# Stick-breaking attention in a two-layer transformer kernel: the causal mask moved from matmuls into the scan, and the values products moved directly behind the scores

## What is computed

```python
rel = query position - key position
strict = rel > 0
z = einsum('bhqd,bhkd->bhqk', q_blk, k) * scale
log_beta = log_sigmoid(z)
log_1mb = where(strict, log_sigmoid(-z), 0.0)
between = cumsum(log_1mb, axis=3, reverse=True) - log_1mb
a = where(strict, exp(log_beta + between), 0.0)
out = einsum('bhqk,bhkd->bhqd', a, v)
```

## Time and profile before

| what | value |
|---|---|
| median of three timed runs | 2841.06 us (2838.6 to 2841.15) |
| profiled execution, first to last instruction (span) | 2839.9 us; the page gives no other time of that execution |
| PE / DVE / ACT / POOL busy | 97% / 58% / 30% / 56% of the span |
| 57 to 336 us (stick-breaking part): PE / DVE / ACT / POOL busy | 271.5 / 168.3 / 136.1 / 161.4 us of 279 |
| mean granted clock of TensorE | 0.990 |

### The profile page before, as it was taken

One profiled execution on the slowest core, in us unless ns is written; L12 is line 12 of the kernel. 1 busy time (PEld: TensorE's weight loads), 2 busy tenths in 40 slices (PEclk: granted clock), 3 DMA queues, 4 the chain that ended last, 5 costly groups with the idle time before them and its releaser, 6 DMA issues.

```text
span 2839.9 us, 38349 instructions
## 1 busy us (share of the span) xinstructions
PE 2742.4 (97%) x13202; PEld 2193.9 (77%) x13202; DVE 1644.7 (58%) x2348; ACT 858.2 (30%) x1696; POOL 1601.4 (56%) x1240
## 2 busy tenths in 40 slices
PE   7999999899999999999999999989999999999998
PEld 5677777676878888887788887767787878888887
DVE  5655577738567777777734302485445355556556
ACT  4544445435321111213413113554233100110102
POOL 3555411355998777776533343222366987777764
PEclk9999999999999999999999999999999999999999
DMA  3322222034211111115411242212424121111134
GB/s 136 102 86 79 87 84 68 23 119 141 82 41 53 56 55 44 59 59 182 167 56 52 74 148 97 82 53 96 171 96 156 37 67 45 53 58 44 59 121 146
DMA packets 76778, 243.77 MB, mean 86 GB/s; under 512 B 7119, under 2 KB 10992, under 8 KB 76276
## 3 DMA queue, kind: packets, MB, share of 16 engines
q1 hardware_dynamic: 54576, 184.31, 19.4%
q10 hardware_dynamic: 22084, 57.86, 5.7%
HBM read 207.00 MB, written 32.52 MB: 84 GB/s over the span
## 4 chain that ended last, share of the span: by engine, by line
PE 81%; DVE 8%; POOL 5%; ACT 3%; issue 2%; DMA 1%; POOLq 0%; DVEq 0%; ACTq 0%; SPq 0%
PE ps L813 17%; PE ps L815 16%; PE ps L814 16%; PE ps L1127 7%; PE ps L1128 7%; PE ps L1129 7%; PE ps L899 2%; PE ps L919 2%; POOL arena L703 1%; PE ps L933 1%; PE ps L1410 1%; PE ps L1422 1%; DVE ps L2489 1%; DVE ps L2506 1%; PE ps L936 1%
## 5 line engine op out<-in xcount | busy, mean ns | idle before, releaser
L639 POOL CAST wh<-raw 128x1024 fp32r<-128x1024 f32 x175 | 186.8, 1067 | 854.4 <-PE ps L815 803.6
L813 PE MATMUL ps<-hh,wh 128*128 128x512 f32 x1456 | 600.6, 412 | 8.1 <-DVE hl L2450 3.6
L815 PE MATMUL ps<-hh,wl 128*128 128x512 f32 x1456 | 572.9, 394 | 0.0
L814 PE MATMUL ps<-hl,wh 128*128 128x512 f32 x1456 | 572.3, 393 | 0.0
L641 POOL TENSOR_TENSOR wl<-raw,wh 128x1024 fp32r<-128x1024 f32 x175 | 422.6, 2415 | 14.0
L729 POOL TENSOR_TENSOR wl<-raw,wh 128x512 fp32r<-128x512 f32 x256 | 344.3, 1345 | 20.5
L813 PEld LDWEIGHTS ps<-hh,wh 128*128 128x128 f32 x1456 | 276.4, 190 | 83.4 <-issue 25.3
L815 PEld LDWEIGHTS ps<-hh,wl 128*128 128x128 f32 x1456 | 275.8, 189 | 60.1
L814 PEld LDWEIGHTS ps<-hl,wh 128*128 128x128 f32 x1456 | 276.6, 190 | 52.7 <-issue 3.4
L813 PE MATMUL ps<-gated,wh 128*128 128x512 f32 (+1 forms) x728 | 279.9, 385 | 3.6 <-DVE gated L2540 3.2
L814 PE MATMUL ps<-gated,wh 128*128 128x512 f32 (+1 forms) x728 | 278.6, 383 | 0.0
(11 more groups left out here) (341 smaller groups left out, 5103.7 us busy)
## 6 DMA issues: line engine op xcount, KB each, us to landing
raw<-weights SPq DMA_DIRECT2D x271, 512.0 KB, 3.5
arena<-w_ada SPq DMA_DIRECT2D x48, 512.0 KB, 3.8
arena<-gate_scratch ACTq DMA_DIRECT2D x20, 512.0 KB, 5.1
arena<-x_t ACTq DMA_DIRECT2D x1, 4096.0 KB, 14.0
x_scratch<-arena ACTq DMA_DIRECT2D x2, 2048.0 KB, 9.0
arena<-x_scratch SPq DMA_DIRECT2D x2, 2048.0 KB, 9.6
gate_scratch<-arena ACTq DMA_DIRECT2D x16, 256.0 KB, 2.1
x_scratch<-arena ACTq DMA_DIRECT2D x1, 4096.0 KB, 12.8
```

The source lines that it names most:

```text
L639: pool.tensor_copy(wh[:, s], raw[:, r]).then_inc(Z.wt_hi, 1)
L813: pe.matmul(out, wh[:, slot, w], xh, start=start, stop=False)
L814: pe.matmul(out, wh[:, slot, w], xl, start=False, stop=False)
L815: return pe.matmul(out, wl[:, slot, w], xh, start=False, stop=stop)
```

## The change

Five edits:

1. The mask products are gone; the scores raise `z_full` themselves. Nothing waits for the mask tile any more in this part of the kernel.
2. A new constant tile `reset` of 128x1024 holds zeros and, in its last 128 columns, the identity. POOL writes it at its start (a memset of 128x896 and a copy of 128x128), ahead of its first split, once the constants are there.
3. The scan is now state = max(u x state, reset), starting at 0, over the keys from right to left. Until the query's own key the state stays 0; there `reset` is 1 and the product starts anew.
4. b is no longer 0 on the last key of the last block, which POOL doesn't multiply. So the last block's values products take 127 keys instead of 128.
5. For stick-breaking steps `a_values` comes directly behind `a_scores`, ahead of the first turn and of fill.

ACT waits once for the mask tile before it stores it for later use. To make room for `reset` in SBUF, the program is created with a DMA scratch of 1024 bytes.

```diff
@@ a_scores (PE)
-                if s == 0:
-                    pe.wait_ge(Z.s_mask, 2)
                         last = pe.matmul(bank(2 * side, 2)[:, c:e], Q_T[i % 2][r, query(s)], K_T[i % 2][r, c:e],
-                                         start=True, stop=(i >= SB_JOBS), skip_group_check=True)
-                        if i >= SB_JOBS and e == w:
+                                         start=True, stop=True, skip_group_check=True)
+                        if e == w:
                             last.then_inc(Z.z_full, 1)
-                if i < SB_JOBS:
-                    for side in range(2):
-                        pe.matmul(bank(2 * side, 2)[:, w - P:w], masks[:, 0], masks[:, 1], start=False, stop=True,
-                                  skip_group_check=True).then_inc(Z.z_full, 1)
@@ a_values (PE)
+                        keys = slice(0, P - 1 if k == b else P)
-                            last = pe.matmul(bank(5)[r, 0:P], HV[i % 2][:, k, r], S_AT[side][s % 2][:, kt],
+                            last = pe.matmul(bank(5)[r, 0:P], HV[i % 2][keys, k, r], S_AT[side][s % 2][keys, kt],
@@ the loop over steps (PE)
                 if s < A_N:
                     a_scores(s)
+                beside = s in VALUES_AT and VALUES_AT[s] < SB_N
+                if beside:
+                    a_values(VALUES_AT[s])
...
                     a_turn(TURN_AT[s], *turning[0])
-                if s in VALUES_AT:
+                if s in VALUES_AT and not beside:
                     a_values(VALUES_AT[s])
@@ POOL, ahead of the first split
+            pool.memset(reset[:, 0:S - P], 0.0).then_inc(Z.s_reset, 1)
+            pool.wait_ge(Z.consts, 32)
+            pool.tensor_copy(reset[:, S - P:S], mat("ident")).then_inc(Z.s_reset, 1)
@@ ACT, ahead of the store of the masks
+            act.wait_ge(Z.s_mask, 2)
@@ s_remain (DVE)
-                v = S_U[u % 3][:, 0:width(s)][:, ::-1]
+                v, ends = S_U[u % 3][:, 0:width(s)][:, ::-1], reset[:, S - width(s):S][:, ::-1]
+                if u == 0:
+                    dve.wait_ge(Z.s_reset, 2)
                 dve.wait_ge(Z.s_u, u + 1)
-                dve.tensor_tensor_scan(v, v, v, 1.0, ALU.mult, ALU.min).then_inc(Z.s_c, 1)
+                dve.tensor_tensor_scan(v, v, ends, 0.0, ALU.mult, ALU.max).then_inc(Z.s_c, 1)
@@ kernel
-    nc = bacc.Bacc("TRN2", target_bir_lowering=False, num_devices=1)
+    nc = bacc.Bacc("TRN2", target_bir_lowering=False, num_devices=1, dynamic_dma_scratch_size=1024)
```

More of the change, by code:

```diff
@@ L156, in build @@
         dsm = place("dsm", [P, 64])
+        reset = place("reset", [P, S])
         ps = ctx.enter_context(nc.psum_tensor("ps", [P, 8 * HALF], F32))
@@ L181, in build @@
         f_half f_ev t_full t_free z_full pv_full o_ev
-        mask_in s_mask s_u s_b s_c s_a d_near d_max d_nmx d_exp d_r d_m d_w
+        mask_in s_mask s_reset s_u s_b s_c s_a d_near d_max d_nmx d_exp d_r d_m d_w
         o_sq o_rs o_norm o_hi o_lo l7_hi l7_lo
```

## The result

The changed kernel takes 2822.41 us (median of 5 runs, 2822.22 to 2824.14), the kernel before 2841.06 us (5 runs, 2836.18 to 2843.83): 18.65 us less, a ratio of 0.994 with an interval of 0.9929 to 0.9951. The forecast was 2826.3 us, with a range of 2820 to 2835.

The account below looks back on a forecast made before the run. PE, busy 97% of the span, was taken to bound the kernel. Masks 8.3, order 4.5 and stalls 2.0 sum to 14.8 us; 2839.9 - 14.8 + 1.2 = 2826.3 us, range 2820 to 2835.

Parts of the forecast that it names:

- PE bounds the stage, and the time follows what it issues: Stick-breaking stage: PE, busy 271.5 of 279 us, sets the time; 14.8 us saved there, the rest shifts whole.
- Masks, 8.3 us: Stick-breaking steps on PE: dropping a pair of mask products saves its 0.277 us slot in 30 steps, 8.3 us.
- Order, 4.5 us at the changes of form and 2.0 at the stalls: Values ahead of the turn: 0.16 us in 28 steps, plus 0.65 us at the turns of steps 9, 17 and 25.
- The rule that a change of tiling mode drains the engine: PE in values steps: one of four mode changes a step goes, a saving; the rule gives no price.
- The chain starts 0.2 us earlier: Chain behind the scores: they signal at their own end, not a mask's, so ACT's sigmoids start 0.2 us earlier.
- A later turn of step 8 costs nothing: Steps 8, 16, 24: ACT's copy and POOL start about 0.9 us later, hidden by overlap with DVE; cost zero.
- Rival B: Masks alone pay; reordering gives nothing and the later copy delays POOL: 8.3 us minus up to 2.7, about 2834 us; chance 0.12.
- The edits at nothing: 127 keys, POOL's memset and copy, the scan's new operands, ACT's mask wait and the smaller DMA scratch: zero cost.
- Rival C: No change: the chain through ACT, DVE and POOL paces a step, PE waits what it saves; 2839 us, chance 0.07.
- Rival D: Slower: DVE's scan with a second stream is slowed beside POOL, 2541 ns to 4.5 us; 2846 us, chance 0.04.
- Per head pair, 4 to 5.5 us and the first 3: Stick-breaking stage: expected shortening of each head pair, 4 to 5.5 us, and 3 us for the first.
- The term without sign: Granted clock drops for short stretches, each costing 1.7 us; shifted work may gain or lose one or two.

Follow-up runs that it names:

- second pair of profiles: Profiles from repeat runs, nothing altered: changed kernel 2821.85 us (ratio 0.9938), kernel before 2837.25 us (ratio 0.9996).
- experiment 1: Changed kernel with the old order, values products behind the first turn again, masks still removed: 2832.76 us against 2840.74 for the kernel before.
- experiment 2: Kernel before with only the new order, values products ahead of the first turn, masks and old scan kept: 2830.75 us, ratio 0.9965.
- experiment 3: Kernel before plus the constant reset tile, which nothing reads, and the smaller DMA scratch: 2840.73 us against 2840.74.
- experiment 6: Changed kernel with 128 instead of 127 keys in the last block's values products: 2820.23 us, ratio 0.9931.
- (4): Changed kernel with DVE copying the transposed values ahead of accumulating the modulation: 2818.79 us, ratio 0.9922.
- (8): Changed kernel with DVE's copy ahead of the accumulation and ACT's exponential table preloaded ahead of its copies: 2818.42 us, ratio 0.9923.
- (7): Changed kernel with DVE's copy first, ACT's exponential table preloaded earlier, and modulation products inside the fill: 2823.51 us, ratio 0.9942.
- (5): Kernel before with the one-column modulation products moved ahead of the last fill groups of their step: 2841.8 us, ratio 1.001.

## Why the prediction was right, step by step

- **PE bounds the stage, and the time follows what it issues: held.** The stage shrank by 15.7 us (15 forecast), 14.0 at full clock (14.8 forecast). That the rest shifts whole held at full clock (within 1 us); by the profiles' own time the rest lost 4.6 us, over the 4 that I had set as a limit, and the lowered stretches (5.2 us) account for it. In the second pair of profiles the rest lost 1.3 us.
- **Masks, 8.3 us: mis-sized as a term by itself.** The slot of 0.27 us is real and additional. But taken alone the masks give 5.5 us (experiment 1), because the wait behind each new pair grew from 1.0 to 1.6 us, three times: 1.8 of the missing 2.8. Most of the other 1.0 is the 0.03 us a step by which the old block is dearer behind scores than behind masks (1.29 against 1.26): some 0.7 us over the 24 steps in which the turn follows them at once and doesn't wait. I had charged such a loss for steps 0 and 1 and not for steps 9, 17 and 25 without the order.
- **Order, 4.5 us at the changes of form and 2.0 at the stalls: somewhat small.** Behind the masks' removal it gives 8.6 us (experiment 1 to the changed kernel). The block took 1.10 us, 0.16 under the earlier trace rows as assumed; 0.19 under experiment 1. The stall went as forecast: 12.08 us from the scores of step 8 to the first fill of step 9 (123.42 to 135.50) against 13.29 (125.16 to 138.45), 1.2 gained, wait 0.72 for the 0.65 that was left over in the working. (The working counted 28 steps for the changes of form; steps 2 to 31 without 9, 17 and 25 are 27, which is 0.2 us.) The two errors, 2.8 too much and 2.1 too little, have one cause and nearly cancel in the sum; for the most part that is no more than luck, since the working had not priced the two edits together: the price of the order had been worked out for a block in which the masks are gone already, and so it holds behind the masks and not by itself (5.1 us, experiment 2).
- **The rule that a change of tiling mode drains the engine** (the Trainium skill, TensorEngine Tiling (Array Packing), Key Properties) had no price and no row of its own. Experiment 2 has the row: the mask pair's 0.27 us become 0.36 ahead of values. The trace agrees with the rule in that a change costs something; the costs differ with the pair of forms (0.06 to 0.21 us), of which the rule says nothing.
- **The chain starts 0.2 us earlier: held**, 2.02 us from the first scores to ACT's sigmoids (123.42 to 125.44) against 2.28, so 0.26.
- **A later turn of step 8 costs nothing: held, with its cover.** ACT's copy starts 5.97 us behind the first scores (129.39) where it was 4.94, and POOL 7.57 (130.99) where it was 6.53, both 1.0 later. POOL's two multiplies then took 5.24 instead of 6.30 us and ended 12.8 us behind the first scores in both kernels, and the accumulation began no later for it (8.0 us behind them in both). All of the difference is in the first multiply, 2.31 instead of 3.36 us: it ended 1.8 us behind the end of DVE's second scan in both. Rival B, which needed 0.9 us here three times, fell.
- **The edits at nothing: held**, the tile and the scratch by experiment 3, the 127 keys by experiment 6.
- **Rival C, no change, fell**: PE's waits did not take up what it saved. It has a true core, in step 1, whose wait grew from 1.11 to 1.55 us, and in experiment 1's step 9.
- **Rival D, the slower scan, fell.** The widest went from 2541 to 2663 ns, 0.12 us where 0.7 would have turned the gain, and all scans together grew by 3.4 us, under the 10 set as a limit. The single scans separate the causes: the second stream costs nothing (2.26 us in both kernels for the second of the two widest, 2012 ns at the next width), and both forms of the scan are held up alike by a POOL instruction that is running when they start. The widest grew because its first scan starts beside a longer rest of POOL's split. Nor is a scan slowed in proportion by POOL's work beside it, as the rival had it: the second scan took 2.26 us with 1.58 us of POOL's multiply beside it before and with 0.53 in the changed kernel.
- **Per head pair, 4 to 5.5 us and the first 3**: measured 4.0, 3.7 and 3.7, and 2.6. The last three sit at or just under the lower end. That band did not fit the sum itself: 14.8 us less 3 for the first pair leave 3.9 for each of the others.
- **The term without sign** decided where the time came out in the range: it came out 3.9 us under the 2826.3, though the work saved was 0.8 us less than forecast. Some 4 us of the 18.65 are granted clock, luck as far as the forecast goes. Some of that, about 2 us between the means over all runs, may belong to the change. In the profiles with the new order the stage has 1 lowered stretch (changed kernel, both profiles), 1 (experiment 2), 0 (4), 1 (6), 1 (8) and 3 (7); with the old order 2 (before), 3 (3), 3 (5) and 0 (1). With one or two executions each and both ends on both sides, it stays open.

## What to carry to other kernels

On an engine that is busy 97% of the time, price a short matmul by the time from its start to the next start, and move products of one tile form next to each other: here 0.27 us for a pair, and 0.06 to 0.21 us for a change of form, added up over 30 steps to a forecast that was 0.8 us off. Before adding up such savings, find the waits that stand behind them, and price edits together where one decides what the other stands next to: these two were worth 14.0 us together and 10.5 as the sum of each alone. And when two kernels differ by half a percent, compare at equal granted clock before looking for a cause of the last few microseconds.

## What the runs showed of the hardware

- The granted clock falls to 0.50 (1.2 instead of 2.4 GHz) for 3.4 us at a time, at some places for twice that, which costs 1.7 us for each. In this kernel it does so at a few places that come again from execution to execution; which of those in the attention part are hit differs (227 us in one profile of before, 208 in the other). A run's mean of 0.989 to 0.993 goes with most of a scatter of 2835 to 2844 us.
- A scan on DVE was not slowed by a POOL instruction that began after it (128x1024: 2.26 us with 0.53 and with 1.58 us of POOL's multiply beside it), and was held up by one that was already running: a scan of 128x256 ended 0.55 us behind the end of that instruction, whether 0.5 or 2.3 us of it were left.
- A change of the tile form cost 0.09 us between masks and values, 0.21 between transposes and values, 0.06 between values and transposes; a contraction over 127 rows instead of 128 nothing (0.37 and 0.36 us to the next group).
- Two multiplies on POOL that were started 1.0 us later took 5.24 instead of 6.30 us. The second took 2.98 us in both kernels; the first ended 1.8 us behind the end of DVE's scan in both, however early it had started. I had expected cover, not a shorter operation. That the first is held up until the scan ends fits these rows; no run tested it.
